# Routing of a product-key mixer: the early expert halves as three fp32r passes of split weights, placed among the heads

## The reference, cut to what matters

```
q = (xi @ w_pq).reshape(TOK_BLOCK, PEER_HEADS, 2, PEER_DQ // 2)
s = jnp.einsum('thcd,hckd->thck', q, sub_keys)
top_s, top_i = lax.top_k(s, PEER_TOPK)
...
best_s, pos = lax.top_k(cand_s, PEER_TOPK)
gate = jax.nn.softmax(best_s, axis=-1)
act = jax.nn.gelu(jnp.einsum('td,thkd->thk', xi, u_tab[idx]))
return jnp.einsum('thk,thkd->td', gate * act, v_tab[idx])
```

## Time and profile before

| | us |
|---|---|
| median of 3 runs | 2670.7 (2670.0 to 2671.6) |
| span of the profiled execution | 2665.9 |
| PE busy | 2488.3 (93%) |
| DVE busy | 2093.9 (79%) |
| ACT busy | 1137.6 (43%) |
| POOL busy | 811.1 (30%) |
| routing stage, from its first matmul to ScalarE's last gelu | 1246 to 1482 |

### The profile page before, as it was taken

One profiled execution on the slowest core, in us unless ns is written; L12 is line 12 of the kernel. 1 busy time (PEld: TensorE's weight loads), 2 busy tenths in 40 slices (PEclk: granted clock), 3 DMA queues, 4 the chain that ended last, 5 costly groups with the idle time before them and its releaser, 6 DMA issues.

```text
span 2665.9 us, 38926 instructions
## 1 busy us (share of the span) xinstructions
PE 2488.3 (93%) x14998; PEld 2188.1 (82%) x14998; DVE 2093.9 (79%) x3683; ACT 1137.6 (43%) x1945; POOL 811.1 (30%) x621
## 2 busy tenths in 40 slices
PE   6889999999999987997999887999999999999997
PEld 5778888888888877996886786888888888888886
DVE  3767777724777765543999796999999999999999
ACT  4335656535666654314444582333333332333333
POOL 0000000004565550100343583443334433343431
PEclk9999999999999988998999998999999999999999
DMA  7421121233233224332123489999999999999996
GB/s 305 174 104 70 68 99 70 86 135 121 84 137 100 86 85 166 140 135 103 65 70 109 151 244 382 417 416 417 416 418 412 418 404 411 405 413 417 417 408 247
DMA packets 166408, 621.48 MB, mean 233 GB/s; under 512 B 14896, under 2 KB 83280, under 8 KB 105808
## 3 DMA queue, kind: packets, MB, share of 16 engines
q1 hardware_dynamic: 124752, 340.03, 34.5%
q0 software_dynamic: 36864, 268.45, 24.5%
q10 hardware_dynamic: 4608, 10.52, 1.3%
HBM read 559.26 MB, written 59.56 MB: 232 GB/s over the span
## 4 chain that ended last, share of the span: by engine, by line
PE 73%; DVE 15%; DMA 5%; ACT 3%; issue 3%; SPq 0%; DVEq 0%; POOL 0%; PEldq 0%; PEld 0%; ACTq 0%; POOLq 0%
PE c_pp L862 8%; PE p_py L2620 5%; PE p_py L2622 5%; PE p_py L2621 5%; PE p_pa L2603 4%; PE p_pa L2605 4%; PE p_pa L2604 4%; PE o_ps L1715 4%; PE s_pg L1407 4%; PE e_ps L2420 4%; PE p_py L2634 3%; DMA w_raw<-in_w_stream 2%; PE g_ps L1070 2%; PE a_ps L810 2%; DVE p_uv L2741 2%
## 5 line engine op out<-in xcount | busy, mean ns | idle before, releaser
L2585 POOL DMA_INDIRECT p_uv<-in_uv_rows,merged x256 | 398.6, 1557 | 619.4 <-DVE merged L2758 558.8
L2603 PE MATMUL p_pa<-h2D,w_hi 128*128 128x384 f32 x896 | 318.8, 356 | 20.6 <-DVE w_lo L2712 20.5
L2758 DVE SCALAR_TENSOR_TENSOR merged<-p_uv,p_sw,merged 128x1024 f32<-128x1024 f32 x256 | 328.7, 1284 | 7.2
L2741 DVE CUSTOM_DVE_ANT_0 p_uv<-p_uv,merged 128x1024 f32<-128x1024 f32 x256 | 308.1, 1220 | 11.3 <-DMA p_uv<-in_uv_rows,merged 11.3
L2605 PE MATMUL p_pa<-h2D,w_lo 128*128 128x384 f32 x896 | 302.8, 338 | 0.0
L2604 PE MATMUL p_pa<-h2D,w_hi 128*128 128x384 f32 x896 | 302.7, 338 | 0.0
L2654 ACT ACTIVATE w_hi<-w_raw 128x2048 fp32r<-128x2048 f32 x110 | 210.4, 1912 | 154.7 <-PE p_py L2622 89.3
L2712 DVE TENSOR_TENSOR w_lo<-w_raw,w_hi 128x2048 fp32r<-128x2048 f32 x110 | 251.8, 2289 | 24.0 <-ACT w_hi L2654 23.7
L2620 PE MATMUL p_py<-w_hi,p_wh 128*128 128x512 f32 x672 | 265.6, 395 | 1.7 <-DVE w_lo L2712 1.7
L2622 PE MATMUL p_py<-w_hi,p_wl 128*128 128x512 f32 x672 | 265.3, 395 | 0.0
L2621 PE MATMUL p_py<-w_lo,p_wh 128*128 128x512 f32 x672 | 265.1, 394 | 0.0
(11 more groups left out here) (408 smaller groups left out, 6101.4 us busy)
## 6 DMA issues: line engine op xcount, KB each, us to landing
w_raw<-in_w_stream SPq DMA_DIRECT2D x174, 1024.0 KB
g_pairs<-e_st SPq DMA_DIRECT2D x5, 4096.0 KB, 16.2
p_g<-g_pairs SPq DMA_DIRECT2D x64, 320.0 KB
t_ada<-in_w_ada SPq DMA_DIRECT2D x16, 1024.0 KB, 7.1
xc_dram<-c_xc SPq DMA_DIRECT2D x8, 1284.0 KB
p_ve<-in_v_early SPq DMA_DIRECT2D x8, 1024.0 KB, 13.4
r_ur<-in_u_early ACTq DMA_DIRECT2D x14, 512.0 KB, 3.7
s_xx<-xc_dram SPq DMA_DIRECT2D x8, 642.0 KB, 6.3
```

Source lines behind the costliest of these rows:

```text
L2585: nc.gpsimd.indirect_dma_start(uv[:, k % RING, :], None, K.uv_rows, bass.IndirectOffsetOnAxis(K.sidx[:, t, c:c + 1], 0)).then_inc(K.gather ...
L2603: nc.tensor.matmul(ps_a[m][:, :], wh[:, k, cols], K.h2D[0][:, k, :], start=k == 0, stop=False)
L2741: nc.vector.tensor_tensor_reduce(uv[:, b, 0:D], uv[:, b, 0:D], K.hrow[:, t, :], 1.0, 0.0, ALU.mult, ALU.add, sa[:, at:at + 1]).then_inc(do ...
L2758: nc.vector.scalar_tensor_tensor(ys[:, t, :], uv[:, b, D:2 * D], sw[:, at:at + 1], ys[:, t, :], ALU.mult, ALU.add).then_inc(v_done, 1)
```

## The change

The early halves are no longer multiplied in float32. ScalarE copies the loaded rows to a high part (`early_hi`, `uh`), POOL subtracts it from the rows for a low part (`early_lo`, `ul`), and PE multiplies high and low with the high and low parts of the activations (`K.h2D`) that the queries use too, in three fp32r passes for each of the 8 blocks. `uh` and `ul` lie in `K.merged_lo`, which is free in this stage. The load of half i + 2 now waits for the subtraction of half i.

The placement changes too. `HELD = (1, 1, 1, 2, 1, 2, 2, 2)` gives how many halves each head holds: the first between its queries and its scores (`behind_queries`), for head 0 as well, the second, where there is one, after its scores (`behind_scores`). That makes 12, and four (`LATE`) remain for the end. POOL's program gets the subtractions between its look-ups: before look-up h those of `behind_scores(h)` and `behind_queries(h + 1)`. ScalarE makes the high part of half i + 2 at the end of the head that holds half i. The replicas and the exp of head 7 stand behind the first and the second late half instead of the third and the fourth.

```diff
--- before.py
+++ after.py
@@ -2061,8 +2061,13 @@
     ps_t = ps_u[1][:, :].rearrange("p (r c) -> p r c", r=3)
     HALVES = 2 * len(EARLY)
 
-    beside = lambda h: range(h - 1, h) if h else range(0)
-    LATE = range(PH - 1, HALVES)
+    HELD = (1, 1, 1, 2, 1, 2, 2, 2)
+    behind_queries = lambda h: range(sum(HELD[:h]), sum(HELD[:h]) + 1)
+    behind_scores = lambda h: range(sum(HELD[:h]) + 1, sum(HELD[:h + 1]))
+    LATE = range(sum(HELD), HALVES)
+    low = K.merged_lo[:, :, :].rearrange("p k t -> p (k t)")
+    uh, ul = ([low[:, (2 * r + m) * KD * P:(2 * r + m + 1) * KD * P].rearrange("p (k c) -> p k c", k=KD) for m in range(2)] for r in range(2))
+    uh_done = sem("r_uh_done"); ul_done = sem("r_ul_done")
     ur = [sb(f"r_ur{m}", [P, KD, P]) for m in range(2)]
     ua = [sb(f"r_ua{m}", [P, TD]) for m in range(2)]
     u_in = [sem("r_u_in0"), sem("r_u_in1")]; u_mm = sem("r_u_mm"); u_ev = sem("r_u_ev"); a_out = [sem("r_a_out0"), sem("r_a_out1")]
@@ -2091,7 +2096,18 @@
     @block.gpsimd
     def _(pool):
         K.enter(pool)
+        def early_lo(i):
+            m = i % 2
+            pool.wait_ge(uh_done, i + 1)
+            if i >= 2:
+                pool.wait_ge(u_mm, i - 1)
+            nc.gpsimd.tensor_tensor(ul[m], ur[m][:, :, :], uh[m].bitcast(F32), ALU.subtract).then_inc(ul_done, 1)
+
+        for i in behind_queries(0):
+            early_lo(i)
         for h in range(LOOKED_UP):
+            for i in list(behind_scores(h)) + list(behind_queries(h + 1)):
+                early_lo(i)
             pool.wait_ge(x_eq, 2 * h + 2)
             pool.wait_ge(fr_done, 2 * h + 2)
             found = eq[:, :, :, :, :].rearrange("p c t e k -> p (c t) (e k)")
@@ -2104,6 +2120,8 @@
             nc.gpsimd.tensor_tensor(slots[:, 0:2, :, TOPK * h:TOPK * (h + 1)], pair[:, :, :, 0:TOPK], pair[:, :, :, TOPK:2 * TOPK],
                                     ALU.add).then_inc(x_done, 1)
             pool.wait_ge(x_done, h + 1)
+        for i in list(behind_scores(PH - 1)) + list(LATE):
+            early_lo(i)
         K.clear_previous(pool)
         K.leave(pool)
 
@@ -2136,21 +2154,22 @@
 
         def early_hidden(i):
             m = i % 2
-            pe.wait_ge(u_in[m], 16 * (i // 2 + 1))
+            pe.wait_ge(ul_done, i + 1)
             if i >= 2:
                 pe.wait_ge(u_ev, i - 1)
             for k in range(KD):
-                mm = nc.tensor.matmul(ps_u[m][:, :], ur[m][:, k, :], K.h32[:, k, :], start=k == 0, stop=k == KD - 1)
+                mm = mm3(nc, ps_u[m][:, :], (uh[m][:, k, :], ul[m][:, k, :]), (K.h2D[0][:, k, :], K.h2D[1][:, k, :]), k == 0, k == KD - 1)
             mm.then_inc(u_mm, 1)
 
-        queries(0, 0)
-        pe.wait_ge(k_in, 16)
-        scores(0, 0)
-        for h in range(1, PH):
+        for h in range(PH):
             queries(h, h % 2)
-            for i in beside(h):
+            for i in behind_queries(h):
                 early_hidden(i)
+            if h == 0:
+                pe.wait_ge(k_in, 16)
             scores(h, h % 2)
+            for i in behind_scores(h):
+                early_hidden(i)
         for i in LATE:
             early_hidden(i)
         pe.wait_ge(x_done, LOOKED_UP)
@@ -2196,10 +2215,18 @@
             act.wait_ge(sub_done, h + 1)
             nc.scalar.activation(be[:, :, :], bs[:, :, :], ACT.Exp).then_inc(be_done, 1)
 
+        def early_hi(i):
+            m = i % 2
+            act.wait_ge(u_in[m], 16 * (i // 2 + 1))
+            if i >= 2:
+                act.wait_ge(u_mm, i - 1)
+            nc.scalar.activation(uh[m], ur[m][:, :, :], ACT.Copy).then_inc(uh_done, 1)
+
         def early_gelu(i):
             m = i % 2
             act.wait_ge(u_mm, i + 1)
             if i + 2 < HALVES:
+                act.wait_ge(ul_done, i + 1)
                 load_early(act, i + 2)
             if i >= 2:
                 act.wait_ge(a_out[m], 16 * (i // 2))
@@ -2207,20 +2234,28 @@
             act.wait_ge(u_ev, i + 1)
             act.dma_start(K.a_dram[i // 2, m], ua[m][:, :]).then_inc(a_out[m], 16)
 
+        early_hi(0)
+        early_hi(1)
         for h in range(PH):
             copies(h, h % 2)
-            for i in beside(h):
+            for i in behind_queries(h):
                 early_gelu(i)
             score_copies(h, h % 2)
             S.hi(act, h + (U_PQ + 2), h % 2)
             if h:
                 replicas(h - 1)
                 gate_exp(h - 1)
+            for i in behind_scores(h):
+                early_gelu(i)
+            for i in range(sum(HELD[:h]), sum(HELD[:h + 1])):
+                early_hi(i + 2)
         for i in LATE:
             early_gelu(i)
-            if i - LATE[0] == 2:
+            if i + 2 < HALVES:
+                early_hi(i + 2)
+            if i - LATE[0] == 0:
                 replicas(PH - 1)
-            if i - LATE[0] == 3:
+            if i - LATE[0] == 1:
                 gate_exp(PH - 1)
         for m in range(2):
             act.wait_ge(a_out[m], 16 * len(EARLY))
```

## The result

The changed kernel takes 2752.8 us in the median of four runs (2749.7 to 2753.9), the kernel before 2670.8. The ratio is 1.0309, with a 95% interval of 1.0297 to 1.0321: slower by 3.1%. The forecast was 2757 us, in a range of 2732 to 2782. The profiled execution has a span of 2748.0 us against 2665.9, 82.1 more.

What follows compares the result with a forecast made beforehand. DVE's unbroken searches were taken to bound the routing, with PE ahead. Start 2.5, HELD = 2 heads 62.4, HELD = 1 heads 4.8 and tail 16.2 sum to 85.9 us: span 2751.8, median 2757 us, range 2732 to 2782.

Steps and rivals of the forecast that it cites:

- The order on POOL decides: In the routing, PE's second halves wait for subtractions queued behind a look-up that can't start before the next search.
- The start, +2.5: Half 0 between the queries and scores of head 0 makes the first search 2.5 us later, never regained.
- A head with HELD = 2, 45.6 us apart: Heads 3, 5 and 6: the next search comes after 45.6 us against 24.8, 20.8 lost each, +62.4 in all.
- my bound of 2.3: POOL's subtraction of 128x1024 was taken as 1.9 us, with 2.3 us as the upper bound.
- The clock: PE's clock falls after a long wait, which costs 2.5 us each time, bounds 0 and 4.
- A head with HELD = 1, 27.2 us apart: Heads 2 and 4: PE's wait for the subtraction delays the scores, 27.2 us against 24.8, +4.8 in all.
- rival C: POOL is slower beside DVE, its subtraction standing still until DVE's weight split is over: 2765, up to 2780 us; chance 25%.
- The last search: The search of head 7 starts at 1510.7 in place of 1440.97, 69.7 us later.
- The tail, +16.2: After the last search starts, late halves go round two buffers and the last ends 56.7 us later, before 40.5.
- then gelu 13, load of 15: In the tail on ScalarE, both follow head 7's replicas, which last until 43.2 us; the load lands at 47.0.
- Rival B: PE's clock stays up through the waits, about 20 us less: 2737 us; chance 12%.
- Rival D: PE never waits for POOL, DVE stays the bound shifted by 2.5 us, four late halves fit: 2662 us; chance 4%.

Runs made afterwards that it cites:

- e1: The changed kernel with POOL's subtractions for behind_scores(h + 1) and behind_queries(h + 2) moved ahead of look-up h: 2676.5 us, ratio 1.0026.
- e3: The changed kernel's placement with the plain float32 product of before, without ScalarE's high copies and POOL's subtractions: 2659.8 us, ratio 0.9963.
- e4: The changed kernel with 104 more matmuls of 128x384 on PE ahead of each of four second halves: 2744.4 us in one timed run.
- e2: The changed kernel with HELD = (1,) * 8, so no second halves and eight late ones: span 2706.4 us.
- e5: e1 with each POOL subtraction replaced by two memsets of the same tile, PE multiplying the high part in the low part's place: span 2667.8 us.
- e6: e1 with each POOL subtraction done twice, one after the other: span 2691.7 us.
- e8: e1 with the first two late halves' subtractions ahead of look-up 6, and head 7's replicas and exp ahead of a load-waiting high copy: 2669.9 us, ratio 1.0005.

## Why the prediction was right, point by point

The main mechanism was right. That the total came within 5 us is in part luck: one term had the right size for the wrong reason, and others cancelled.

- **The order on POOL decides: right.** e1 moves only the order and takes back 69.9 of 82.1 us; e3 takes the wait away and is faster than before.
- **The start, +2.5:** search 0 began at 1270.2 against 1267.6, +2.6.
- **A head with HELD = 2, 45.6 us apart:** measured 43.3, 45.8 and 45.2. Three times 20.8 was forecast, 18.5 + 21.0 + 20.4 = 59.9 measured against 62.4. Look-ups 4 and 5 start 4.2 us after searches 5 and 6, where I had put 4.1. Look-up 2 starts only 2.3 us after search 3, since the score copies that ScalarE's chain starts from had ended 1.9 us before DVE was free. That is most of why the first is short.
- **Inside that chain two terms were off and cancelled.** POOL's subtraction was 2.34 us at its shortest and 2.48 in the mean, above even my bound of 2.3; two of them at 1253.48, with DVE idle, took 4.76, so this is its own price and not DVE's. The estimate by the multiply with float32 output was the wrong neighbour: doubling the fp32r row gave 2.26. The clock cost 1.2 to 1.9 us for a long wait (e4), where I had put 2.5.
- **A head with HELD = 1, 27.2 us apart: 27.2 and 28.6 measured, but the first agrees by luck.** The forecast has DVE waiting there for scores that PE's wait for the subtraction makes late. Before search 3 DVE did not wait: PE's chain had the copies ready 25.3 us after search 2 (look-up 1 had begun at 1322.09, 2.0 us after search 2 and not 4.1), and the 27.2 are DVE's own sums beside POOL, which is rival C. Before search 5 both come out alike: the copies ended at 1419.15, and DVE's own work, with 3.6 us of standing still at the sums and the cast, at 1419.07. e2 has only heads of this kind, and DVE waits for scores in none of them behind the first. So this step of the forecast, the wait for scores in heads with HELD = 1, failed for search 3, and its 2.4 us were rival C's. The gap from search 1 to search 2, counted at nothing, was 0.8 us longer than before, and that is rival C too.
- **The last search:** forecast at 1510.7, measured at 1510.2.
- **The tail, +16.2: mis-sized, +13.9.** The last half ended some 54.4 us after the last search began and not 56.7. It started when I had said, 49.9 us after the search against 50.0. The term that failed is the low clock that I charged to it "after some 3 us of idling": PE had waited 0.18 us, the granted clock was 1.00, and the half took 4.5 us and not 6.7. PE had not idled because half 14 had started 2.6 us later than forecast, 45.3 us after the search, and half 15 directly behind it. Half 15 could do that because "then gelu 13, load of 15" behind the replicas was wrong as well: the load was issued at 1552.26, as soon as half 13 had ended and before the replicas ran. So here too errors cancelled. The rows of ScalarE and PE:

```profile
1552.03 1.06 ACT L2223 ACTIVATE merged_lo<-r_ur 128x1024 fp32r<-128x1024 f32 x1 [3.05 <-DMA r_ur<-in_u_early]
1552.26 0.33 ACTq L2082 DMA_DIRECT2D r_ur<-in_u_early  x1
1552.99 2.41 ACT L2212 ACTIVATE r_fr<-r_f 128x1280 bf16<-128x1280 bf16 x2
...
1560.17 0.44 PE L121 MATMUL r_pu<-h2D,merged_lo 128*128 128x384 f32 x1 [0.18 <-POOL merged_lo L2104]
```

- **Rival C, POOL beside DVE, 25%: the price of running together is real, its place was another.** I had looked for it at the weight split, which no subtraction met on the path here. DVE paid at the small sums and the cast instead. Here the sums of head 3 and the subtraction that began among them, from DVE's timeline and POOL's:

```profile
1359.60 3.14 DVE L2292 TENSOR_TENSOR r_cand<-r_v 128x120 f32<-128x120 f32 x4
```

  Four sums that took 0.70 us took 3.14 and ended 0.1 us after the subtraction that began at 1360.30. The cast took 1253 ns in the mean against 243 before. In all DVE was busy for 224.9 us in the stage against 198.5, 26.4 more. Before searches 2 and 3 that cost 0.8 and 2.4 us; most of the rest cost nothing, because DVE would have waited for scores anyway. In e1, where DVE is the bound again, it counts in full: its last search comes 8.2 us later than e3's. The rule of the Trainium skill ("SBUF — State Buffer", section "Who interferes with whom"), that a DVE instruction with two SBUF inputs contends with a GpSimd instruction that reads SBUF, agrees with e5 and e6. The same section says that a cast can use the shared pair too, which agrees with the cast held up by memsets in e5.
- **Rival B, the clock stays up: out** in the changed kernel (granted clock 0.59, 0.50). e4 made it so by other work, and the span fell by 5.3, the stage by 7.7.
- **Rival D, no wait for POOL:** 2662 was forecast for it. e1 brings about what I saw no way to, by moving the subtractions, and took 2676.5: D has DVE's pace untouched and the last four halves done beside the search, and e1 has neither. e3, which has no wait and no split, took 2659.8; it confirms the placement and not D's sum.

Sum: 2.6 + 0.8 + 2.4 + 18.5 + 3.8 + 21.0 + 20.4 + 13.9, about 83.4 by the gaps between the searches, of which the last stage gave back 1.5.

## What to carry to other kernels

Work given to an idle engine is placed in that engine's queue: ask what stands ahead of it there, when that can start, and what is queued behind the instruction that waits for it. POOL was 30% busy, and where its 2.5 us subtractions stood in its queue made up 74 of the 83 us that the stage lost, because they stood behind a look-up that can start only when DVE is at the next search, and PE was meant to be ahead of that search. A distance that comes out as forecast doesn't show the mechanism: look who waited. And look whether the work that is made cheaper is on the path at all: the passes saved PE 1 us of 5 where PE had nine to spare, while placing the halves, untouched by the split, was worth 0.4% by itself.

## What the runs showed of the hardware that I had not expected

- A POOL subtraction of 128x1024 to fp32r takes 2.34 to 2.42 us where nothing holds it, with DVE idle too, a multiply of that size to float32 1.90. A memset of 128x1024 takes 0.95:

```profile
L2104 POOL MEMSET merged_lo<- 128x1024 f32 x16 | 15.3, 953 | 166.1 <-ACT merged_lo L2226 165.7
```

- A DVE sum of two SBUF tensors that starts while POOL subtracts is held until POOL's instruction ends, however small it is: a sum of 128x40, 0.19 us alone, took 1.80 in the mean of e6. DVE's other instructions aren't all held: its reduction and reciprocal behind the sums kept their 0.2 us beside e1's subtractions. The other way round POOL is held: in e8 a subtraction that started 0.05 us behind DVE's weight split took 4.43 us and ended 2.20 us after the split had, so the one that comes second stands still. e6 has two more such meetings, with 4.48 and 4.43 us.

```profile
1468.39 2.28 DVE L111 TENSOR_TENSOR w_lo<-w_raw,w_hi 128x2048 fp32r<-128x2048 f32 x1
1470.59 0.72 DVE L2281 MAX8 r_bv<-r_cand 128x8 f32<-128x64 f32 x5
...
1468.44 4.43 POOL L2104 TENSOR_TENSOR merged_lo<-r_ur,merged_lo 128x1024 fp32r<-128x1024 f32 x1
```

- A cast with one input was held up by POOL's memset: 0.88 us in e5 beside the second of two.

```profile
1360.38 0.88 DVE L2302 CAST r_f<-r_i 128x160 bf16<-128x160 uint32 x1
...
1360.21 0.95 POOL L2106 MEMSET merged_lo<- 128x1024 f32 x1
```

- ScalarE's queue issued a load 0.7 us ahead of an activation that stands before it in the program (1552.26 against 1552.99 above).
